# Mixture-of-experts blocks of a two-layer trunk on Trainium2: input rows loaded two blocks ahead and copied into place by GpSimd

## Chip, cores and metric

One Trainium2 chip, one core, float32 throughout. The metric is the time of the whole program on the device, in microseconds (us); less is better. The engines are named as the profile names them: PE (TensorE), DVE (VectorE), ACT (ScalarE), POOL (GpSimd) and SP (SyncE, which only issues DMAs here); a "q" behind a name is the engine's sequencer.

## The reference

Two layers of a diffusion backbone run over 128 context and 256 latent tokens of width 1024. Each layer is a mixer (attention in the first, long convolution in the second), a layer norm, a mixture of experts and a layer norm. What matters here is the mixture of experts, with 16 experts of inner width 512, two of which are chosen for each of the 384 tokens:

```
hg = t @ w_gate[e];  hu = t @ w_up[e]
act = silu(hg) * hu * comb[:, e]
y = sum_e act @ w_down[e]
```

An expert's three matrices are 2 MB each, so a layer reads 96 MB of them; the tokens are 1.5 MB.

## The kernel before

**Slots.** After the router, POOL scatters each token's row twice by indirect DMA (L469) into a DRAM tensor, slot_rows, at a place sorted by expert; each expert's rows are padded to blocks of BLK = 32. `table` holds where each expert's blocks begin, and its last entry is the number of blocks, which depends on the data. slot_rows was filled with zeros near the start of the program (L1217).

**The loop over blocks.** Each engine runs its own loop of that many trips, and they meet by semaphores alone.

- POOL (`pool_moe`) waits until PE has transposed the rows of a block (rowT_mm) and then loads the next block's 32 rows, as 64 half rows, from slot_rows into slot_in (L475). There is one such buffer.
- PE (`pe_moe`) waits for row_in and transposes slot_in into a PSUM bank (L733, in `rows_to_channels`); does the 64 gate and up matmuls of a block (L740); transposes the next block's rows while ACT and DVE make the activation; then does the 32 down matmuls (L747).
- ACT (`act_moe`) applies Silu (L1038, with a table load before it), and copies half of the result from PSUM into slot_out (L1041). Then it stores slot_out into slot_rows by two DMAs (L1045), over the rows that the block was read from.
- DVE (`dve_moe`) copies the transposed rows out of PSUM (L1114), multiplies and transposes the activation (L1119, L1121), and copies the other half of the result (L1135). L1041 and L1135 both wait for slot_stored: the store of the block before must have landed, since there is one slot_out.
- SP (`load_moe`) streams the weights through nine places of 2 MB, three experts deep (L416). A place is filled again when PE's last use of it is over. So an expert's loads are issued when the expert three before it is done.

**Around the loop.** In POOL's program, the wait for down_mm of the last expert but one and a small addition (L484) follow the loop, then `ln_rows` (four loads of 512 KB for the next layer norm, L440 to L442), waits for the last row load and the last store, an addition (L490), and six gathers of the result rows (L494). ACT's L953 and DVE's L982 to L988 work on what the gathers bring. POOL's L451 is a layer norm's addition.

Of the kernel before, what the change touches and what calls it, by code (L numbers as in the profile page):

```python
# [15 lines left out]
F32 = mybir.dt.float32  # L16
# [6 lines left out]
D = 1024  # L23
# [138 lines left out]
def trunk_program(nc, a, out):  # L162

    ctx = ExitStack()
    with ctx:
# [13 lines left out]
        idx = sb("idx", [P, 2 * NT], I32)  # L179
        table = sb("table", [1, NE + 1], I32)  # L180
        ada_bias = sb("ada_bias", [P, 512])
        bank = [ctx.enter_context(nc.psum_tensor(f"bank{i}", [P, 512], F32))[:, :] for i in range(8)]

        slots = nc.dram_tensor("slot_rows", [(MAX_BLOCKS + 2) * BLK, D], F32).ap()

# [80 lines left out]
        act_T = at(4096, FT, BLK)  # L266
        slot_out = at(4224, 512, rows=2 * BLK)
        SPARE = 7168
        picked = at(8192, NT, 2, D)
# [25 lines left out]
        def rt(k, *dims):  # L295
# [46 lines left out]
        rlog_mm, rscore, htok_mm, htok_act = [sem(n) for n in ("rlog_mm", "rscore", "htok_mm", "htok_act")]  # L342
        mask_rdy, pos_mm, table_rdy, idx_rdy, zero_rdy, zeroed, scattered, ln_first = [sem(n) for n in (
            "mask_ready", "pos_mm", "table_ready", "idx_ready", "zero_ready", "zeroed", "scattered", "rows_scaled")]
        MS = [{n: sem(f"{n}_{layer}") for n in (
            "row_in", "rowT_mm", "rowT", "gu_mm", "silu", "gated", "act", "down_mm", "evac_dve", "evac_act",
            "slot_stored")} for layer in range(2)]
# [113 lines left out]
        def pool_moe(pool, l):  # L461
            S = MS[l]
            pool.wait_ge(idx_rdy, 2 * (l + 1))
            pool.wait_ge(htok_act, 6 * (l + 1))
            if l == 0:
                pool.wait_ge(zeroed, 16 * ZERO_DMAS)
            for r in range(2):
                for t in range(NT):
                    pool.indirect_dma_start(slots[:, :], bass.IndirectOffsetOnAxis(ap=idx[:, r * NT + t:r * NT + t + 1], axis=0),  # L469
                                            h_tok[:, t, :], None).then_inc(scattered, 16)  # L470
            pool.wait_ge(table_rdy, l + 1)
            blocks = pool.value_load(table[0:1, NE:NE + 1], min_val=NE, max_val=MAX_BLOCKS)
            pool.wait_ge(scattered, 16 * 6 * (l + 1))
            def row_halves(block):
                pool.dma_start(slot_in, slots[bass.ds(block * BLK, BLK), :].rearrange("s (h c) -> (s h) c", h=2)).then_inc(S["row_in"], 16)  # L475

            row_halves(0)
            with pool.Fori(1, blocks + 1) as b:
                pool.wait_ge(S["rowT_mm"], b)
                row_halves(b)  # L480

            before_last = pool.value_load(table[0:1, NE - 1:NE], min_val=NE - 1, max_val=MAX_BLOCKS)
            pool.wait_ge(S["down_mm"], before_last)
            pool.tensor_tensor(idle, wsel[:, 0, 0:1], wsel[:, 0, 0:1], ALU.add).then_inc(idle_set, 1)  # L484
            pool.wait_ge(idle_set, 2 * l + 1)
            ln_rows(pool, 2 * l + 1)
            pool.wait_ge(S["row_in"], blocks * 16 + 16)
            pool.wait_ge(S["slot_stored"], blocks * 32 + 32)
            pool.wait_ge(S["rowT"], blocks + 1)
            pool.tensor_tensor(idle, wsel[:, 0, 0:1], wsel[:, 0, 0:1], ALU.add).then_inc(idle_set, 1)  # L490
            pool.wait_ge(idle_set, 2 * l + 2)
            for t in range(NT):
                for r in range(2):
                    pool.indirect_dma_start(picked[:, t, r, :], None, slots[:, :],  # L494
                                            bass.IndirectOffsetOnAxis(ap=idx[:, r * NT + t:r * NT + t + 1], axis=0)).then_inc(gathered[t], 16)
# [206 lines left out]
        def pe_moe(pe, l, first):  # L702
# [26 lines left out]
            def rows_to_channels():  # L729

                wait_counted(pe, S["row_in"], rows_due, 16)
                for j in range(4):
# [34 lines left out]

            rows_due = counter(pe, f"rows_due{l}", 16)
            rows_to_channels()
# [131 lines left out]
        MIX_DMAS = 3  # L901
        ZERO_STEP = 6
        ZERO_DMAS = (MAX_BLOCKS + 2) // ZERO_STEP
        CONST_ALL = 16 * 6
# [143 lines left out]
        def dve_moe(dve, link, l):  # L1048
# [58 lines left out]
            for r, oh in enumerate((oh0, oh1)):  # L1107
                link(dve.tensor_tensor(eq, oh, soff, ALU.mult))
                link(dve.tensor_reduce(slot_f[:, r, :], eq, AX, ALU.add))
                dve.tensor_copy(idx[:, r * NT:(r + 1) * NT], slot_f[:, r, :]).then_inc(idx_rdy, 1)  # L1110
            dve.wait_ge(table_rdy, l + 1)
            blocks = dve.value_load(table[0:1, NE:NE + 1], min_val=NE, max_val=MAX_BLOCKS)
# [11 lines left out]
            dve.sem_inc(S["evac_dve"], 1)  # L1124
            dve.wait_ge(S["rowT_mm"], 1)
            rows_in()
            with dve.Fori(0, blocks) as b:
                dve.wait_ge(S["silu"], b + 1)
                gated(b, 0)
                gated(b, 1)  # L1130
                dve.wait_ge(S["rowT_mm"], b + 2)
                rows_in()
# [71 lines left out]
        def gpsimd_program(pool):  # L1204
# [10 lines left out]
            rows = slots.rearrange("(b r) n -> r b n", r=BLK)  # L1215
            for b in range(0, MAX_BLOCKS + 2, ZERO_STEP):
                pool.dma_start(rows[:, b:b + ZERO_STEP, :],  # L1217
# [458 lines left out]
```

## Time and profile before

| what | value |
|---|---|
| device time, median of 3 runs | 1385.99 us (1384.95 to 1388.35) |
| device time of the profiled execution | 1387.69 us |
| its span, first to last instruction | 1386.0 us |
| granted clock of PE, mean | 0.884 |
| PE busy | 1025.2 us (74%) |
| DVE busy | 412.2 us (30%) |
| ACT busy | 262.3 us (19%) |
| POOL busy | 107.8 us (8%) |
| moved by DMA | 343.83 MB, 248 GB/s over the span |

A profile is one execution. Busy shares are means over stages with different limits; what a wait costs is read from the chain of work that ended last, which is followed back from the last instruction, at each step to what released it. A line such as `PE L733 MATMUL bank<-keep,arena` names engine, line, operation and the tensors written and read; slot_in, slot_out, slot_ahead and the other buffers of the loop all lie in `arena`. In a timeline, the brackets at a line's end hold how long the engine had been idle and what released it. Times are microseconds from the start of the span.

### The profile page before, as it was taken

The page shows a single profiled execution, that of the slowest core. Times are in us where ns is not written, and L with a number is a line of the kernel's source. Part 1 is how long each engine was busy: PE and PEld are TensorE (multiplying, and loading weights), DVE is VectorE, ACT ScalarE, POOL GpSimd, SP SyncE. Part 2 cuts the span into 40 slices and gives each one's busy share as a digit, 9 for nine tenths or more (in the row PEclk, how much of TensorE's full clock was granted, in tenths as well). Part 3 has the DMA queues.
Part 4 walks back from the last instruction along what each step waited for, and adds up shares of the span by engine and source line. Part 5 has one row for each costly group of instructions (what it writes and reads, how often), then busy time and mean ns, then how long its engine had stood idle before and what let it go on. Part 6 is the DMA issues. An engine that isn't in the chain of part 4 may idle for free.

```text
span 1386.0 us, 23542 instructions
## 1 busy us (share of the span) xinstructions
PE 1025.2 (74%) x9358; PEld 573.8 (41%) x9358; DVE 412.2 (30%) x1120; ACT 262.3 (19%) x456; POOL 107.8 (8%) x168
## 2 busy tenths in 40 slices
PE   1899996896368655778569999889748788876540
PEld 0444455645234323444235554435434444443220
DVE  0310128806211111112354234551631222111106
ACT  0401012502122211223122111110222222222111
POOL 1100001100200000000220000000010000000012
PEclk9999998996699878999879999999858999988785
DMA  9975334394396999993995104636421938799983
GB/s 322 372 255 182 129 117 150 120 426 167 121 386 231 390 411 404 401 349 128 348 377 217 61 16 139 240 122 262 163 93 36 369 129 328 275 396 404 411 338 136
DMA packets 78264, 343.83 MB, mean 248 GB/s; under 512 B 7783, under 2 KB 8362, under 8 KB 65917
## 3 DMA queue, kind: packets, MB, share of 16 engines
q1 hardware_dynamic: 57108, 289.16, 54.0%
q0 software_dynamic: 13152, 42.92, 9.0%
q10 hardware_dynamic: 7944, 10.88, 2.4%
q8 instruction: 47, 0.77, 0.2%
q14 instruction: 13, 0.10, 0.0%
HBM read 319.70 MB, written 23.23 MB: 247 GB/s over the span
## 4 chain that ended last, share of the span: by engine, by line
PE 43%; DMA 34%; DVE 11%; issue 6%; ACT 2%; SPq 2%; ACTq 1%; POOL 1%; POOLq 0%; DVEq 0%
DMA slot_rows<-arena 11%; PE bank L575 10%; PE bank L800 9%; PE bank L740 7%; DMA arena<-in_moe_w_up_dram 6%; DMA arena<-slot_rows 5%; DMA ring<-in_moe_w_up_dram 5%; DMA ring<-in_ada_w_dram 4%; PE bank L747 4%; PE bank L698 3%; DMA arena<-in_ln_b_dram 2%; PE bank L528 2%; SPq L1151 1%; PE bank L874 1%; PE bank L897 1%
## 5 line engine op out<-in xcount | busy, mean ns | idle before, releaser
L740 PE MATMUL bank<-ring,arena 128*32 128x256 f32 x3008 | 189.1, 408 | 35.0 <-DMA ring<-in_moe_w_up_dram 32.8
L740 PEld LDWEIGHTS bank<-ring,arena 128*32 128x32 f32 x3008 | 103.1, 119 | 116.8 <-issue 60.3
L575 PE MATMUL bank<-ring,hT 128*128 128x512 f32 x336 | 144.9, 593 | 1.0 <-ACT hT L933 1.0
L800 PE MATMUL bank<-hT,ring 128*128 128x384 f32 x384 | 124.6, 487 | 1.0 <-ACT hT L933 1.0
L747 PE MATMUL bank<-ring,arena 128*32 128x256 f32 x1504 | 105.7, 428 | 23.5 <-DVE arena L1121 23.5
L1119 DVE TENSOR_TENSOR arena<-arena,bank 128x64 f32<-128x64 f32 x134 | 27.0, 201 | 287.8 <-ACT arena L1038 287.8
L733 PE MATMUL bank<-keep,arena 64*128 64x64 f32 x276 | 31.9, 239 | 103.6 <-DMA arena<-slot_rows 103.6
L1038 ACT ACT_TABLE_LOAD x67 | 86.0, 1283 | 105.6 <-issue 97.5
L740 PE MATMUL bank<-arena 128*32 128x256 f32 x1280 | 82.7, 416 | 24.6 <-DMA arena<-in_moe_w_up_dram 24.6
L575 PEld LDWEIGHTS bank<-ring,hT 128*128 128x128 f32 x336 | 63.6, 190 | 80.5 <-issue 79.3
L800 PEld LDWEIGHTS bank<-hT,ring 128*128 128x128 f32 x384 | 72.7, 190 | 52.5 <-ACT hT L933 1.2
L528 PE MATMUL bank<-ring,small 128*32 128x256 f32 x768 | 52.7, 435 | 56.2 <-DMA ring<-in_ada_w_dram 54.9
L1135 DVE COPY arena<-bank 64x256 f32<-64x256 f32 x67 | 27.9, 416 | 177.2 <-DMA slot_rows<-arena 121.8
L1041 ACT ACTIVATE arena<-bank 64x256 f32<-64x256 f32 x67 | 25.5, 381 | 287.5 <-DMA slot_rows<-arena 181.8
L475 POOL DMA_DIRECT2D arena<-slot_rows x69 | 36.2, 525 | 552.7 <-PE bank L733 545.2
L733 PEld LDWEIGHTS bank<-keep,arena 64*128 64x128 f32 x276 | 23.2, 144 | 132.8 <-issue 132.8
L747 PEld LDWEIGHTS bank<-ring,arena 128*32 128x32 f32 x1504 | 48.6, 120 | 59.9 <-DVE arena L1121 27.6
L740 PEld LDWEIGHTS bank<-arena 128*32 128x32 f32 x1280 | 44.8, 121 | 60.7 <-issue 39.3
L528 PEld LDWEIGHTS bank<-ring,small 128*32 128x32 f32 x768 | 28.5, 125 | 78.9 <-issue 68.1
L747 PE MATMUL bank<-arena 128*32 128x256 f32 x640 | 48.6, 455 | 11.5 <-DVE arena L1121 11.5
L1114 DVE COPY arena<-bank 128x256 f32<-128x256 f32 x69 | 27.7, 401 | 55.8 <-PE bank L733 55.4
L698 PE MATMUL bank<-ring,arena 128*128 128x512 f32 x96 | 41.5, 593 | 1.3 <-DVE arena L1647 1.3
(285 smaller groups left out, 1014.1 us busy)
## 6 DMA issues: line engine op xcount, KB each, us to landing
ring<-in_ada_w_dram SPq DMA_DIRECT2D x24, 2048.0 KB, 15.2
ring<-in_moe_w_gate_dram SPq DMA_DIRECT2D x22, 2048.0 KB, 20.9
ring<-in_moe_w_up_dram SPq DMA_DIRECT2D x22, 2048.0 KB, 23.9
ring<-in_moe_w_down_dram SPq DMA_DIRECT2D x22, 2048.0 KB, 25.4
arena<-in_moe_w_gate_dram SPq DMA_DIRECT2D x10, 2048.0 KB, 24.0
arena<-in_moe_w_up_dram SPq DMA_DIRECT2D x10, 2048.0 KB, 29.3
arena<-in_moe_w_down_dram SPq DMA_DIRECT2D x10, 2048.0 KB, 29.6
ring<-in_ev_w_in_dram SPq DMA_DIRECT2D x7, 2048.0 KB, 15.7
```

Source lines behind the costliest of these rows:

```text
L475: pool.dma_start(slot_in, slots[bass.ds(block * BLK, BLK), :].rearrange("s (h c) -> (s h) c", h=2)).then_inc(S["row_in"], 16)
L528: pe.matmul(b[32 * j:32 * j + 32, 0:HALF], condT[:, 2 * k:2 * k + 32], slot8(chunks[j // 2])[:, k, j % 2 * HALF:j % 2 * HALF + HALF], star ...
L575: last = pe.matmul(bank[3 * (c % 2) + t], hT[:, k, t * P:(t + 1) * P], slot8(n)[:, k, :], start=k == 0, stop=k == KT - 1)
L698: last = pe.matmul(bank[2 * t + half], src[:, k, t * P:(t + 1) * P], slot8(n0 + half)[:, k, :], start=k == 0, stop=k == KT - 1)
L733: last = pe.transpose(bank[0][:, j * 2 * BLK:(j + 1) * 2 * BLK], slot_in[:, j * P:(j + 1) * P], ident[0:2 * BLK, 0:2 * BLK])
L740: last = pe.matmul(bank[1][q * BLK:(q + 1) * BLK, 0:HALF], slot_inT[:, k, :], both[:, :, k, q * P:(q + 1) * P], start=k == 0, stop=k == KT ...
L747: last = pe.matmul(bank[5][tile * BLK:(tile + 1) * BLK, 0:HALF], act_T[:, f, :], slot4(s + 2)[:, f, q * HALF:(q + 1) * HALF], start=f == 0 ...
L800: last = pe.matmul(bank[c % 3][:, 0:T], slot8(n)[:, k, (c % 4) * P:(c % 4 + 1) * P], hT[:, k, :], start=k == 0, stop=k == KT - 1)
L1038: act.activation(silu_g, bank[1][:, 0:P].rearrange("p (r f) -> p f r", f=FT), ACT.Silu).then_inc(S["silu"], 1)
L1114: return dve.tensor_copy(slot_inT.rearrange("p (h j) s -> p h j s", h=2), bank[0][:, 0:HALF].rearrange("p (j s h) -> p h j s", j=4, h=2)). ...
L1119: dve.tensor_tensor(act_rows[:, two, :], silu_g[:, two, :], up, ALU.mult).then_inc(S["gated"], 1)
L1135: dve.tensor_copy(slot_out[:, 0:HALF], bank[5][0:2 * BLK, 0:HALF]).then_inc(S["evac_dve"], 1)
```

## The change

Two buffers of 64x512, slot_ahead, take the row loads. The first two blocks are loaded before the loop. In each step POOL waits for the load of this block and for PE's transposes of the block before, does an addition on one column, copies the buffer into slot_in (row_rdy, which PE now waits for), waits for that copy, and issues the load of the block two further on into the same buffer. The loop is in pairs of blocks, so the number of trips is not the number of blocks: DVE works out blocks / 2 rounded down, plus 1, after the table, into `trips`. rowT_mm starts from 1, so DVE's waits on it are one higher. slot_rows is two blocks longer, and the zero fill goes in eleven steps of four blocks instead of seven of six.

```diff
@@ -178,10 +178,11 @@
...
         table = sb("table", [1, NE + 1], I32)
+        trips = sb("trips", [1, 1], I32)
         ada_bias = sb("ada_bias", [P, 512])
...
-        slots = nc.dram_tensor("slot_rows", [(MAX_BLOCKS + 2) * BLK, D], F32).ap()
+        slots = nc.dram_tensor("slot_rows", [(MAX_BLOCKS + 4) * BLK, D], F32).ap()
@@ -265,6 +266,7 @@
...
         slot_out = at(4224, 512, rows=2 * BLK)
+        slot_ahead = [at(5376, 512, rows=2 * BLK), at(5888, 512, rows=2 * BLK)]
         SPARE = 7168
@@ -340,10 +342,10 @@
...
         rlog_mm, rscore, htok_mm, htok_act = [sem(n) for n in ("rlog_mm", "rscore", "htok_mm", "htok_act")]
-        mask_rdy, pos_mm, table_rdy, idx_rdy, zero_rdy, zeroed, scattered, ln_first = [sem(n) for n in (
-            "mask_ready", "pos_mm", "table_ready", "idx_ready", "zero_ready", "zeroed", "scattered", "rows_scaled")]
+        mask_rdy, pos_mm, table_rdy, idx_rdy, zero_rdy, trips_rdy, zeroed, scattered, ln_first = [sem(n) for n in (
+            "mask_ready", "pos_mm", "table_ready", "idx_ready", "zero_ready", "trips_ready", "zeroed", "scattered", "rows_scaled")]
         MS = [{n: sem(f"{n}_{layer}") for n in (
-            "row_in", "rowT_mm", "rowT", "gu_mm", "silu", "gated", "act", "down_mm", "evac_dve", "evac_act",
+            "row_in0", "row_in1", "row_rdy", "rowT_mm", "rowT", "gu_mm", "silu", "gated", "act", "down_mm", "evac_dve", "evac_act",
             "slot_stored")} for layer in range(2)]
@@ -470,21 +472,31 @@
...
             blocks = pool.value_load(table[0:1, NE:NE + 1], min_val=NE, max_val=MAX_BLOCKS)
+            pool.wait_ge(trips_rdy, l + 1)
+            pairs = pool.value_load(trips[0:1, 0:1], min_val=NE // 2 + 1, max_val=MAX_BLOCKS // 2 + 1)
             pool.wait_ge(scattered, 16 * 6 * (l + 1))
-            def row_halves(block):
-                pool.dma_start(slot_in, slots[bass.ds(block * BLK, BLK), :].rearrange("s (h c) -> (s h) c", h=2)).then_inc(S["row_in"], 16)
-
-            row_halves(0)
-            with pool.Fori(1, blocks + 1) as b:
-                pool.wait_ge(S["rowT_mm"], b)
-                row_halves(b)
+
+            def rows_ahead(block, odd):
+                pool.dma_start(slot_ahead[odd], slots[bass.ds(block * BLK, BLK), :].rearrange("s (h c) -> (s h) c", h=2)).then_inc(S[f"row_in{odd}"], 16)
+
+            rows_ahead(0, 0)
+            rows_ahead(1, 1)
+            with pool.Fori(0, pairs) as pair:
+                for odd in range(2):
+                    pool.wait_ge(S[f"row_in{odd}"], pair * 16 + 16)
+                    pool.wait_ge(S["rowT_mm"], pair * 2 + (odd + 1))
+                    pool.tensor_tensor(idle, wsel[:, 0, 0:1], wsel[:, 0, 0:1], ALU.add)
+                    pool.tensor_copy(slot_in, slot_ahead[odd]).then_inc(S["row_rdy"], 1)
+                    pool.wait_ge(S["row_rdy"], pair * 2 + (odd + 1))
+                    rows_ahead(pair * 2 + (odd + 2), odd)
...
             ln_rows(pool, 2 * l + 1)
-            pool.wait_ge(S["row_in"], blocks * 16 + 16)
+            for odd in range(2):
+                pool.wait_ge(S[f"row_in{odd}"], pairs * 16 + 16)
             pool.wait_ge(S["slot_stored"], blocks * 32 + 32)
@@ -728,7 +740,7 @@
...
-                wait_counted(pe, S["row_in"], rows_due, 16)
+                wait_counted(pe, S["row_rdy"], rows_due, 1)
                 for j in range(4):
@@ -765,7 +777,8 @@
...
-            rows_due = counter(pe, f"rows_due{l}", 16)
+            rows_due = counter(pe, f"rows_due{l}", 1)
+            pe.sem_inc(S["rowT_mm"], 1)
             rows_to_channels()
@@ -899,8 +912,8 @@
...
         MIX_DMAS = 3
-        ZERO_STEP = 6
-        ZERO_DMAS = (MAX_BLOCKS + 2) // ZERO_STEP
+        ZERO_STEP = 4
+        ZERO_DMAS = (MAX_BLOCKS + 4) // ZERO_STEP
         CONST_ALL = 16 * 6
@@ -1108,6 +1121,11 @@
...
                 dve.tensor_copy(idx[:, r * NT:(r + 1) * NT], slot_f[:, r, :]).then_inc(idx_rdy, 1)
+            pairs_f = rt(12, 1)
+            link(dve.tensor_scalar(pairs_f, base[:, NE:NE + 1], 0.5, 0.75, ALU.mult, ALU.add))
+            link(dve.tensor_scalar(pairs_f, pairs_f, ROUND, None, ALU.add))
+            link(dve.tensor_scalar(pairs_f, pairs_f, ROUND, None, ALU.subtract))
+            dve.tensor_copy(trips[0:1, :], pairs_f[0:1, :]).then_inc(trips_rdy, 1)
             dve.wait_ge(table_rdy, l + 1)
@@ -1122,13 +1140,13 @@
...
             dve.sem_inc(S["evac_dve"], 1)
-            dve.wait_ge(S["rowT_mm"], 1)
+            dve.wait_ge(S["rowT_mm"], 2)
             rows_in()
...
                 gated(b, 1)
-                dve.wait_ge(S["rowT_mm"], b + 2)
+                dve.wait_ge(S["rowT_mm"], b + 3)
                 rows_in()
@@ -1213,7 +1231,7 @@
...
             rows = slots.rearrange("(b r) n -> r b n", r=BLK)
-            for b in range(0, MAX_BLOCKS + 2, ZERO_STEP):
+            for b in range(0, MAX_BLOCKS + 4, ZERO_STEP):
                 pool.dma_start(rows[:, b:b + ZERO_STEP, :],
...
```

## Rows read from the trace of the kernel before

**Rows 1.** The page's part 4, the chain that ended last, shares of the span by line.

```profile
DMA slot_rows<-arena 11%; PE bank L575 10%; PE bank L800 9%; PE bank L740 7%; DMA arena<-in_moe_w_up_dram 6%; DMA arena<-slot_rows 5%; DMA ring<-in_moe_w_up_dram 5%; DMA ring<-in_ada_w_dram 4%; PE bank L747 4%; PE bank L698 3%; DMA arena<-in_ln_b_dram 2%; PE bank L528 2%; SPq L1151 1%; PE bank L874 1%; PE bank L897 1%
```

**Rows 2.** Who waited for whom: us in total, times, longest.

```profile
DVE arena L1135 <- DMA slot_rows<-arena: 121.8, 33, 5.6
...
PE bank L733 <- DMA arena<-slot_rows: 103.6, 36, 19.8
```

**Rows 3.** DMA issues: times, KB each, median us from issue to landing.

```profile
slot_rows<-arena ACTq DMA_DIRECT2D x134, 64.0 KB, 6.4
```

**Rows 4.** Timeline, 645 to 653, no weights in flight: start us, us, instruction.

```profile
645.10 0.46 PE L733 MATMUL bank<-keep,arena 64*128 64x64 f32 x4
...
645.80 0.24 DVE L1121 STREAM_TRANSPOSE arena<-arena 128x64 f32<-128x64 f32 x1
...
646.11 1.93 PE L747 MATMUL bank<-ring,arena 128*32 128x256 f32 x32 [0.54 <-DVE arena L1121]
...
646.36 0.39 DVE L1114 COPY arena<-bank 128x256 f32<-128x256 f32 x1
647.86 3.64 PE L740 MATMUL bank<-ring,arena 128*32 128x256 f32 x64
...
651.42 0.46 PE L733 MATMUL bank<-keep,arena 64*128 64x64 f32 x4
```

**Rows 5.** The chain in order of time, 376 to 430: start us, us, what.

```profile
388.43 8.54 DMA arena<-slot_rows
...
401.48 0.43 DVE arena L1135
...
428.67 0.43 DVE arena L1135
```

**Rows 6.** Timeline, 376 to 403, VectorE's L1135.

```profile
380.69 0.42 DVE L1135 COPY arena<-bank 64x256 f32<-64x256 f32 x1 [1.46 <-PE bank L747]
...
390.01 0.42 DVE L1135 COPY arena<-bank 64x256 f32<-64x256 f32 x1 [1.78 <-DMA slot_rows<-arena]
```

**Rows 7.** Windows: us, busy of PE, PEld, DVE, ACT, POOL, PEclk, DMA share, GB/s.

```profile
1190.00:1330.00 140.00, 94.57 (x1324) 49.45 (x1316) 20.69 (x79) 25.61 (x40) 7.06 (x15) 0.83 1.00 402
```

**Rows 8.** POOL's groups: busy us, mean ns, idle before.

```profile
L451 POOL TENSOR_TENSOR x<-arena 128x1024 f32<-128x1024 f32 x3 | 9.0, 2991 | 73.7 <-DVE arena L1018 73.7
...
L1213 POOL MEMSET arena<- 32x1024 f32 x1 | 0.9, 943 | 42.5 <-PE bank L1268 42.5
```

**Rows 9.** The chain in order of time, 340 to 700.

```profile
364.33 3.69 issue
...
552.35 7.80 DMA arena<-slot_rows
...
564.14 0.43 DVE arena L1135
...
601.83 8.77 DMA arena<-slot_rows
```

**Rows 10.** The row loads of layer 1, by their line, 1000 to 1386.

```profile
L475 POOL DMA_DIRECT2D arena<-slot_rows x35: 522/522/580, 1038.0 to 1327.6; - x35
```

**Rows 11.** Timeline of PE, 1285 to 1348.

```profile
1321.37 5.16 PE L740 MATMUL bank<-arena 128*32 128x256 f32 x64 [6.92 <-DMA arena<-in_moe_w_up_dram]
...
1338.28 5.24 PE L740 MATMUL bank<-ring,arena 128*32 128x256 f32 x64 [8.87 <-DMA ring<-in_moe_w_up_dram]
```

**Rows 12.** Timeline, 1324 to 1386, POOL, ScalarE and VectorE.

```profile
1330.01 1.20 POOL L440 DMA_DIRECT2D arena<-gate_rows  x2 [0.30 <-POOL small L484]
...
1356.82 1.15 ACT L953 ACTIVATE arena<-arena,small 128x1024 f32<-128x1024 f32 x1 [9.90 <-DMA arena<-slot_rows,idx]
...
1359.43 1.22 DVE L983 TENSOR_TENSOR arena<-arena 128x1024 f32<-128x1024 f32 x1
...
1371.68 3.31 POOL L451 TENSOR_TENSOR x<-arena 128x1024 f32<-128x1024 f32 x1 [14.26 <-DVE arena L1018]
1372.83 3.25 DVE L983 TENSOR_TENSOR arena<-arena 128x1024 f32<-128x1024 f32 x1
```

## The prediction

> **What bounds the kernel now.** I read the chain of work that ended last first, because busy shares say nothing about a wait. The experts' loop puts three things on it [rows 1]: the weight DMAs, the DMA that stores a block's output rows (slot_rows<-arena, 11% of the span) and, with 5%, the DMA that loads a block's input rows (arena<-slot_rows), which is what the change attacks. The waits give the same contest from the engines' side [rows 2]: TensorE stood idle 103.6 us before the transposes of L733 for that load, but VectorE's L1135, the copy of the result into slot_out, stood 121.8 us for the store before it. Both are round trips of one buffer through one DMA; a store lands 6.4 us after its issue in the median [rows 3].
>
> Next the timeline of a block while no weights are in flight [rows 4]. The 64 gate and up matmuls take 3.64 us, the transposes of the next rows 0.46, the activation ends in L1121, the down matmuls take 1.93, and from L733 of one block to that of the next (645.10, 651.42) it is 6.3 us. PE waits for no rows there, and nothing can be won.
>
> While weights are in flight the row load takes 8.5 us [rows 5] and the store as long: L1135 runs at 380.69 and 390.01 [rows 6], 9.3 us apart, and from 401.48 to 428.67 the chain makes three rounds of store and L1135 in 27.2 us, 9.06 each [rows 5]. A round of rows (0.45 of transposes, 0.55 of issue, 7 to 8.5 of DMA) is 8.0 to 9.5 us. So **two loops of nearly equal length run side by side**, and the change opens only the one that is mostly hidden by the other.
>
> Last the windows [rows 7]: from 1190 to 1330 the DMA share is 1.01 at 402 GB/s. There the weights' own bytes set the pace, and a faster block merely waits longer.
>
> **Part by part.** The base is the profiled execution, 1387.69 us for a span of 1386.0; the median of the runs shown is 1385.99, so 1.7 lower, and I count changes against either.
>
> 1. *Start of each layer's loop.* Rows of block 0 used to land where PE takes them. Now POOL waits, does a one-column addition (0.2), a gap and the 64x512 copy before PE may start. The copy is not in the trace. Lower end: half of the 1024-column memset of L1213, 0.47 us. Upper end: half of L451's addition of 1024 columns, 2.99 in the mean, so 1.5 [rows 8]. A copy reads one operand where the addition reads two, so I take the middle, 1.0. With 0.2 and some 0.3 of gaps: **+1.5 us a layer, +3.0 together** (2.0 to 4.0). The Trainium skill (GPSIMD Engine Reference, on its per-element model) has 769 ns for a tight loop over 512 elements; by that the two starts would cost 2.5 instead of 3.0.
>
> 2. *First contended blocks, layer 0.* Row load 388.43 + 8.54 holds PE until L1135 can only run at 401.48 [rows 5]. With rows ready the store loop ends the wait: 390.01 plus a round of 9.3 [rows 6] is 399.3. **-2.2.** From 401.48 on the chain is stores alone; nothing more comes there.
>
> 3. *Around 552.* The load 552.35 + 7.80 delays L1135 to 564.14 [rows 9]. The transposes before that load began 1.05 before 552.35, so by the block of [rows 4] (L733, 1.0 later L747, its 1.93 and 0.1) L1135 ran at 554.3; a store round of 9.06 on is 563.4, and with rows at hand nothing else is late. **-0.8.** Again stores follow.
>
> 4. *From 601.83 on*, four row loads in a row are on the chain, 8.77 us the first [rows 9]. But in that stretch the results wait for stores too, and the block period ahead is bounded by the store round; I follow the blocks one by one with the store landings held fixed and get half a microsecond at the end of it. **-0.5** (0 to -2).
>
> 5. *Layer 1.* One row load is on the chain, near 1190, just when the DMA share reaches 1.01 and stays there for 140 us [rows 7]: **0**. The later start counts in full, as it delays the release of the first ring buffers.
>
> 6. *POOL's tail, layer 1.* This is the step that is moved. Layer 1 had 35 row loads [rows 10], so 34 blocks; an even number makes one trip more than PE uses, and its copy waits for the last transposes (end of the L740 of 1338.28, 1343.5 and 0.45 [rows 11]). All that POOL has behind it waits as well: the wait for down_mm, L484, and the four 512 KB loads of ln_rows, which were issued from 1330.01 [rows 12]. They move to 1343.9 + 1.5 + 0.6 for the last row load + 1.1 for the table value and L484, so 1347.1. Two effects. They leave the way of the last weights: the last L740 began 16.9 us after the one before it [rows 11], where 6.55 MB for an expert and its rows at 402 GB/s [rows 7] is 16.3: **-0.6**. And 2.1 MB stand in POOL's queue ahead of the gathers: at 402 GB/s 5.2 us, from about 1348.5 to 1353.7; two gathers of 512 KB and a landing of 2 us later it is 1358.3, where ScalarE's first L953 began at 1356.82 [rows 12]: **+2.0** after allowing for the pace of the later gathers (0, if they hide, to +5.2, if all of it stands ahead).
>
> 7. *The rest.* Eleven zero fills of 512 KB replace seven of 768 KB: 0.26 MB more, 0.65 us at 402 GB/s in a stretch with weights, of which I take **+0.3**. VectorE has four more small operations and POOL one more table value before the loop; they lie beside POOL's wait of 3.69 us for the scatters [rows 9], and cost about 0.5 us if that cover went. In the steady loop POOL does copy, wait and issue in some 2.3 us of the 6.3 of a block, and PE needs the copy only at the end of the next block: nothing. A load is issued one transposition plus 1.6 us later and is wanted two blocks on, over 12 us, against 8.8 for the longest load: PE's wait for rows should go almost whole. Layer 0 has 33 blocks, so no extra trip.
>
> Sum: +3.0 -2.2 -0.8 -0.5 -0.6 +2.0 +0.3 = **+1.2**, so 1388.9 for a profiled execution and 1387 for a median. What is late in place of the rows is the store before.
>
> **Rivals.** *Faster, because stores get quicker.* Row loads would be issued about 2 us earlier in a block than now, and if a store thereby took 0.8 us less, some 18 of the 33 waits of L1135 [rows 2] would shrink, if those in saturated stretches like that of [rows 7] are left out: -14, 1373. For it: both use the same DMA engines and overlap. Against: one row load per store still overlaps it. 0.17.
>
> *Faster, PE's wait is the price.* If the 103.6 us that L733 stood idle [rows 2] were on the path, the kernel would come to 1283. Against: the chain has 5% for that DMA, and each of its pieces ends beside a store. 0.03.
>
> *Slower, the copy holds up VectorE.* L983 took 3.25 us beside POOL's L451 of 3.31, and 1.22 without it [rows 12]. If POOL's copy, which comes as L1121 and L1114 run [rows 4], blocked them for its full 1.0 us, the second L1121 would end 0.35 us after the down matmuls want it; over some 17 blocks at the 6.3 us pace that is +6, 1393. It decides from a delay of about 0.65 us on. 0.10. The Trainium skill (SBUF — State Buffer, "Who interferes with whom") says that a VectorE instruction contends with a GpSimd one that reads SBUF if it has two SBUF inputs or runs in a 2-port mode; L983 has two, in agreement with its 3.25, and the loop's operations have one, so by that rule this rival gives 0 in place of +6.
>
> *Slower, the moved ln_rows.* If the gathers wait for the whole 5.2 us in POOL's queue and the copy is at its upper end (+1.0), it is 1387 + 3.2 + 1.0 = 1391.2. It decides when the gathers come over 5 us late. 0.13.
>
> **Chances.** A measurement of this kernel tells about 0.3%, 4.2 us, from no change. The forecast, 1382 to 1391, has 0.57; faster 0.17 + 0.03 = 0.20; slower 0.10 + 0.13 = 0.23. The range leaves out the far end of both sides: 1374 to 1395.
>
> **What the profile would show.** Right: L733's wait for rows near zero, now for a POOL copy of about 1 us; L1135's wait for stores grown, above 140 us; slot_rows<-arena with more of the chain, arena<-slot_rows gone; the first L740 of each layer 1.5 us later; ln_rows issued near 1347. Wrong: a store median well under 6.4 us, a block without weights in flight at other than 6.3 us, or L1135 waiting no longer than before while the layers end many microseconds sooner.

## The result, and the profile after

The changed kernel takes 1399.96 us (median of 4 runs, 1396.3 to 1401.74) where the kernel before, run beside it, took 1387.17 (1384.95 to 1390.42): a ratio of 1.0087, with an interval of 1.0057 to 1.0117. Two more sets gave 1.0037 and 1.0067 (below). It is slower, by 5 to 13 us, and the forecast of no change is wrong. The profiled run took 1396.3 us for a span of 1394.6, 8.6 us above the one before.

The page's part 4, the chain that ended last, by line:

```profile
DMA slot_rows<-arena 15%; PE bank L587 10%; PE bank L813 9%; PE bank L752 8%; DMA arena<-in_moe_w_up_dram 6%; DMA ring<-in_moe_w_up_dram 5%; DMA ring<-in_ada_w_dram 5%; PE bank L759 4%; PE bank L710 3%; DMA arena<-in_ln_b_dram 2%; PE bank L540 2%; ACTq L1058 1%; SPq L1169 1%; PE bank L887 1%; PE bank L910 1%
```

The row load arena<-slot_rows, 5% in [rows 1], is gone from it. The store slot_rows<-arena had 11% and has 15%. The two together were 16% and are 15%: the chain has changed its route, and the two DMAs have kept their share of it.

The waits of the changed kernel (us in total, times, longest). L745 is the transposes' line (before L733), L752 gate and up, L759 the down matmuls, L1139 the transposed activation, L1153 and L1054 the two copies of the result into slot_out, L489 POOL's new copy:

```profile
POOL small L488 <- PE bank L745: 463.7, 66, 17.2
...
ACT arena L1054 <- DMA slot_rows<-arena: 198.6, 35, 7.2
DVE arena L1153 <- DMA slot_rows<-arena: 155.6, 35, 6.0
...
PE bank L759 <- DVE arena L1139: 98.1, 67, 4.7
...
PE bank L745 <- POOL arena L489: 41.1, 2, 20.7
```

TensorE no longer waits for rows inside the loop: the 41.1 us before its transposes are the two starts of the layers, which lie in the 103.6 us of [rows 2] too. The idle time has gone one step down the block. In the kernel before this line was

```profile
PE bank L747 <- DVE arena L1121: 35.0, 40, 2.9
```

so before the down matmuls it was 35.0 us in 40 times and is 98.1 in 67; before transposes and down matmuls together it was 103.6 + 35.0 = 138.6 and is 41.1 + 98.1 = **139.2 us**. The copy of the result waits 155.6 us for the store before it, where [rows 2] have 121.8: an earlier result reaches a slot_out that is no earlier free.

Why a late store holds TensorE at the down matmuls shows in ScalarE's order of work. From the timeline at 624 (L1054 is its copy of the result, L1051 the Silu of the next block):

```profile
624.05 0.38 ACT L1054 ACTIVATE arena<-bank 64x256 f32<-64x256 f32 x1 [5.93 <-DMA slot_rows<-arena]
...
626.06 1.28 ACT L1051 ACT_TABLE_LOAD   x1 [1.62 <-issue]
627.35 0.28 ACT L1051 ACTIVATE arena<-bank 128x128 f32<-128x128 f32 x1
```

ScalarE stands in its copy until the store has landed, then issues the next store, loads its table and only then applies Silu. The next block's gate/up was done at 624.1, its down matmuls begin at 628.22. So the store's wait reaches TensorE through ScalarE, whether or not the rows are there. (Silu before the copy was not tried.)

The chain in order of time from 376 to 430 (start us, us, what), the stretch of [rows 5, 6]:

```profile
383.15 8.54 DMA slot_rows<-arena
391.71 0.43 DVE arena L1153
...
392.83 8.33 DMA slot_rows<-arena
401.18 0.43 DVE arena L1153
...
402.29 7.37 DMA slot_rows<-arena
...
410.79 7.70 DMA slot_rows<-arena
...
419.62 9.11 DMA slot_rows<-arena
428.76 0.43 DVE arena L1153
```

Each store is followed by the next result's copy, and that by the next store; gate/up, transposes and down matmuls hide behind them. The last copy in it starts at 428.76; before it was at 428.67.

POOL's new instructions, by line (busy us, mean ns | idle before), and the store in the list of DMA issues, where [rows 3] have 6.4 us:

```profile
L489 POOL COPY arena<-arena 64x512 f32<-64x512 f32 x70 | 42.0, 601 | 0.0
...
L488 POOL TENSOR_TENSOR small<-small 128x1 f32<-128x1 f32 x70 | 13.2, 188 | 466.9 <-PE bank L745 463.7 <-DMA arena<-slot_rows 3.3
```

```profile
slot_rows<-arena ACTq DMA_DIRECT2D x134, 64.0 KB, 6.1
```

And a block without weights in flight, from the timeline of 640 to 656, to stand beside [rows 4]:

```profile
643.45 0.60 POOL L489 COPY arena<-arena 64x512 f32<-64x512 f32 x1
643.47 0.24 DVE L1139 STREAM_TRANSPOSE arena<-arena 128x64 f32<-128x64 f32 x1
...
643.77 1.93 PE L759 MATMUL bank<-ring,arena 128*32 128x256 f32 x32 [0.54 <-DVE arena L1139]
...
649.09 0.46 PE L745 MATMUL bank<-keep,arena 64*128 64x64 f32 x4
...
655.41 0.46 PE L745 MATMUL bank<-keep,arena 64*128 64x64 f32 x4
```

The period is 6.32 us as before. L489 runs in the same 0.6 us as L1139, and L1139 still takes 0.24 with the down matmuls 0.54 behind it: with no weights in flight the copy costs nothing.

**Stages.** The first and last instructions of the stages, read from the timelines of several profiles, give this table (us; the mean where there are several profiles, with their ends):

```
                               before, 2 profiles     after, 3 profiles
scatters -> transposes, L0     13.7                   14.9
loop of layer 0 (33 blocks)    294.3 (293.3, 295.2)   297.6 (295.7 to 298.6)
untouched stretch up to L1     352.1 (352.0, 352.2)   354.8 (353.8 to 356.5)
scatters -> transposes, L1     13.8                   14.7
loop of layer 1 (34 blocks)    305.9 (304.4, 307.3)   305.7 (302.9 to 307.4)
last result copy -> gathers    3.6                    6.8
span                           1387.0                 1397.5
```

A loop is counted from the first gate/up matmul to the start of the last result copy. Three things are plain: the layers start 1.2 and 0.9 us later, the gathers of layer 1 come 3.2 us later behind the last result, and the loops between won nothing. That is 5.3 us of the 10.5. The rest is in layer 0's loop and in a stretch whose instructions the change doesn't touch. These two rows are the loosest of the table: the run before_late_lnrows below, which is the kernel before up to the end of layer 1, has 293.7 us for that loop and 354.1 for that stretch, and exact_trips, which is the changed kernel up to there, 295.6 and 353.8.

Part of the difference has a place. From the first gather of layer 0 to TensorE's second group of matmuls on in_ada_w, the weights that are loaded behind the experts', it is 36.3, 36.4 and 37.1 us in the three profiles with the old loop and 38.8, 38.9 and 39.0 in the three of the changed kernel. The chain waits there for the first of these weights: 18.0 us before, 22.1 after.

```profile
665.16 17.95 DMA ring<-in_ada_w_dram
```

```profile
669.16 22.14 DMA ring<-in_ada_w_dram
```

Why that load lands later, no run shows.

### The profile page after: what moved, and what is told of

It reads as the page before. It is cut to its first block, busy times and chain, and to the rows that moved or that the text cites. A ratio compares the mean times of both kernels' runs of the same rounds, so it can differ in the third digit from the quotient of the medians.

```text
span 1394.6 us, 23687 instructions
## 1 busy us (share of the span) xinstructions
PE 1027.1 (74%) x9358; PEld 573.2 (41%) x9358; DVE 410.6 (29%) x1128; ACT 262.6 (19%) x456; POOL 163.5 (12%) x317
## 4 chain that ended last, share of the span: by engine, by line
PE 43%; DMA 34%; DVE 11%; issue 5%; ACT 3%; ACTq 1%; SPq 1%; POOL 1%; POOLq 0%; DVEq 0%
DMA slot_rows<-arena 15%; PE bank L587 10%; PE bank L813 9%; PE bank L752 8%; DMA arena<-in_moe_w_up_dram 6%; DMA ring<-in_moe_w_up_dram 5%; DMA ring<-in_ada_w_dram 5%; PE bank L759 4%; PE bank L710 3%; DMA arena<-in_ln_b_dram 2%; PE bank L540 2%; ACTq L1058 1%; SPq L1169 1%; PE bank L887 1%; PE bank L910 1%
## 5 line engine op out<-in xcount | busy, mean ns | idle before, releaser
L752 PE MATMUL bank<-ring,arena 128*32 128x256 f32 x3008 | 192.1, 413 | 37.8 <-DMA ring<-in_moe_w_up_dram 35.6
L752 PEld LDWEIGHTS bank<-ring,arena 128*32 128x32 f32 x3008 | 104.2, 120 | 122.1 <-issue 67.3
L759 PE MATMUL bank<-ring,arena 128*32 128x256 f32 x1504 | 104.1, 423 | 61.4 <-DVE arena L1139 61.4
L752 PE MATMUL bank<-arena 128*32 128x256 f32 x1280 | 83.8, 420 | 24.2 <-DMA arena<-in_moe_w_up_dram 24.2
L1153 DVE COPY arena<-bank 64x256 f32<-64x256 f32 x67 | 27.9, 417 | 205.6 <-DMA slot_rows<-arena 155.6
L759 PEld LDWEIGHTS bank<-ring,arena 128*32 128x32 f32 x1504 | 47.9, 118 | 98.0 <-DVE arena L1139 67.8
L1054 ACT ACTIVATE arena<-bank 64x256 f32<-64x256 f32 x67 | 25.6, 382 | 287.5 <-DMA slot_rows<-arena 198.6
L759 PE MATMUL bank<-arena 128*32 128x256 f32 x640 | 48.0, 451 | 36.7 <-DVE arena L1139 36.7
L752 PEld LDWEIGHTS bank<-arena 128*32 128x32 f32 x1280 | 45.0, 122 | 61.3 <-issue 40.2
L488 POOL TENSOR_TENSOR small<-small 128x1 f32<-128x1 f32 x70 | 13.2, 188 | 466.9 <-PE bank L745 463.7
L745 PE MATMUL bank<-keep,arena 64*128 64x64 f32 x276 | 32.1, 237 | 41.1 <-POOL arena L489 41.1
L745 PEld LDWEIGHTS bank<-keep,arena 64*128 64x128 f32 x276 | 22.6, 140 | 68.8 <-issue 68.8
L480 POOL DMA_DIRECT2D arena<-slot_rows x74 | 39.0, 528 | 55.3 <-POOL arena L489 46.8
L759 PEld LDWEIGHTS bank<-arena 128*32 128x32 f32 x640 | 21.2, 124 | 54.0 <-DVE arena L1139 39.5
```

The source lines that it names most:

```text
L480: pool.dma_start(slot_ahead[odd], slots[bass.ds(block * BLK, BLK), :].rearrange("s (h c) -> (s h) c", h=2)).then_inc(S[f"row_in{odd}"], 16)
L745: last = pe.transpose(bank[0][:, j * 2 * BLK:(j + 1) * 2 * BLK], slot_in[:, j * P:(j + 1) * P], ident[0:2 * BLK, 0:2 * BLK])
L752: last = pe.matmul(bank[1][q * BLK:(q + 1) * BLK, 0:HALF], slot_inT[:, k, :], both[:, :, k, q * P:(q + 1) * P], start=k == 0, stop=k == KT ...
L759: last = pe.matmul(bank[5][tile * BLK:(tile + 1) * BLK, 0:HALF], act_T[:, f, :], slot4(s + 2)[:, f, q * HALF:(q + 1) * HALF], start=f == 0 ...
L1054: act.activation(slot_out[:, HALF:2 * HALF], bank[5][2 * BLK:4 * BLK, 0:HALF], ACT.Copy).then_inc(S["evac_act"], 1)
L1153: dve.tensor_copy(slot_out[:, 0:HALF], bank[5][0:2 * BLK, 0:HALF]).then_inc(S["evac_dve"], 1)
```

## Experiments

**The changed kernel again**, twice (no edit).

> The changed kernel once more, as the yardstick for the others. Every theory: between 1396 and 1402 us, 9 to 15 us above the kernel before; its profile shows again first scatter to first transposes some 1.0 to 1.2 us longer a layer, and the last copy of the result to the first gather 6.8 us instead of 3.6 in layer 1.

Measured: 1397.22 us (12 runs) against 1390.34 (35 runs), ratio 1.0037 (1.0015 to 1.0060). The time is in the range; 7 us above the kernel before is less than the 9 to 15 expected. The two stages came again as expected (14.9 and 14.8 us at the starts, 6.7 at the end).

> The changed kernel again, on another set of runs. Theory A (two first copies of 1.1 us and the moved ln_rows with 3.2 us, no gain in the loops): 4 to 8 us above the kernel before. Rival B (a cost of 10 us or more, of which half is in the loops): 10 us or more above it.

Measured: 1398.25 us (7 runs) against 1388.66 (24 runs), ratio 1.0067 (1.0044 to 1.0090). With 9.6 us it lies between the two theories (4 to 8, and 10 or more) and decides for neither. The slowdown is real in all three sets; its size moves between 5 and 13 us.

**The kernel before again**, as a measure of what such a comparison tells.

> The kernel before, run as if it were an experiment: it shows what a difference of nothing looks like in twelve runs. Every theory: a ratio within 0.3% of 1. Its profile is a second sample of each stage: stages in which nothing is changed should differ from the first profile's by no more than some 2 us.

Measured: 1389.17 us (12 runs), 1.0007 (0.9984 to 1.0029), so an interval of 0.2% on either side. Its layer 1 loop took 307.3 us where the first profile has 304.4: a single profile says nothing about 3 us in a loop.

**No extra trip in layer 1.** POOL makes 17 pairs for 33 blocks, as the changed kernel does, and 17 instead of 18 for 34. PE's last transposes, whose result nothing uses, are let through by one more raise of row_rdy behind POOL's loop.

```diff
+            pool.sem_inc(S["row_rdy"], 1)
...
-            link(dve.tensor_scalar(pairs_f, base[:, NE:NE + 1], 0.5, 0.75, ALU.mult, ALU.add))
+            link(dve.tensor_scalar(pairs_f, base[:, NE:NE + 1], 0.5, 0.25, ALU.mult, ALU.add))
```

> POOL's loop makes no trip more than there are rows to copy (17 pairs in both layers), so ln_rows of layer 1 is issued under the last expert again. Theory A (the moved ln_rows stands before the last block's store and the gathers): 3 us less than the changed kernel, last copy of the result to first gather back at 3.6 us, 1393 to 1398. Rival B (the cost lies in the loop, in POOL's copy beside VectorE or in later row loads): no change beyond 1 us. Rival C (ln_rows merely takes time from the last weights instead): the layer's last weights land 1 us later and at most 2 us are won.

Measured: 1393.25 us (12 runs), 1.0026 (0.9997 to 1.0055), 4.0 less than the changed kernel run beside it; 3 were expected. The end of layer 1 is where the profiles differ. First the kernel before, 1346 to 1351:

```profile
1346.56 0.42 DVE L1135 COPY arena<-bank 64x256 f32<-64x256 f32 x1 [1.46 <-PE bank L747]
1347.18 0.80 ACTq L1045 DMA_DIRECT2D slot_rows<-arena  x2
1349.44 0.19 POOL L490 TENSOR_TENSOR small<-small 128x1 f32<-128x1 f32 x1 [17.19 <-DMA slot_rows<-arena]
1350.15 1.01 POOL L494 DMA_INDIRECT arena<-slot_rows,idx  x1 [0.53 <-POOL small L490]
```

Then the changed kernel's timeline, 1349 to 1359:

```profile
1349.34 0.60 POOL L489 COPY arena<-arena 64x512 f32<-64x512 f32 x1
...
1352.00 1.12 POOL L442 DMA_DIRECT2D arena<-gate_rows  x2 [0.47 <-POOL small L495]
1352.33 0.80 ACTq L1058 DMA_DIRECT2D slot_rows<-arena  x2
...
1353.63 0.53 POOL L444 DMA_DIRECT2D arena<-in_ln_b_dram  x1
1357.82 0.19 POOL L502 TENSOR_TENSOR small<-small 128x1 f32<-128x1 f32 x1 [3.66 <-DMA slot_rows<-arena]
1358.53 1.03 POOL L506 DMA_INDIRECT arena<-slot_rows,idx  x1 [0.52 <-POOL small L502]
```

And the same place without the extra trip:

```profile
1339.14 1.12 POOL L442 DMA_DIRECT2D arena<-gate_rows  x2 [0.30 <-POOL small L496]
...
1355.17 0.80 ACTq L1059 DMA_DIRECT2D slot_rows<-arena  x2
...
1357.41 0.19 POOL L503 TENSOR_TENSOR small<-small 128x1 f32<-128x1 f32 x1 [16.11 <-DMA slot_rows<-arena]
1358.32 1.03 POOL L507 DMA_INDIRECT arena<-slot_rows,idx  x1 [0.72 <-POOL small L503]
```

With the extra trip the 2 MB of ln_rows are issued in the same microsecond as the last store (1352.00 and 1352.33), and 5.5 us pass from that store's issue to L502, which waits for it (1352.33 to 1357.82); without it 2.2 (1355.17 to 1357.41). From the last result copy to the first gather it is 6.8 us against 3.8. The gathers are not held by ln_rows in POOL's queue: from the first of them to ScalarE's first use of what they bring (L953, L966 here) it is 6.8 us (1358.53 to 1365.37), and 6.7 in the kernel before (1350.15 to 1356.82).

**The kernel before with ln_rows late**: that step alone.

```diff
             pool.wait_ge(S["down_mm"], before_last)
+            if l == 1:
+                pool.wait_ge(S["rowT_mm"], blocks + 1)
```

> The kernel before with that one step of the change alone: in layer 1 POOL waits for the last transposes before ln_rows. Theory A: 3 us slower than before, 1389 to 1392, with last copy of the result to first gather 6.5 to 7 us. Rivals B and C: within 1 us of the kernel before.

Its timeline at the same place:

```profile
1347.83 0.53 POOL L442 DMA_DIRECT2D arena<-in_ln_b_dram  x1
...
1348.82 0.86 ACTq L1047 DMA_DIRECT2D slot_rows<-arena  x2
1354.49 0.19 POOL L492 TENSOR_TENSOR small<-small 128x1 f32<-128x1 f32 x1 [6.14 <-DMA slot_rows<-arena]
```

The store again takes 5.7 us to L492, and the stage is 6.8 us: the +3.2 is reproduced without any other part of the change. The total doesn't show it, 1391.08 us (12 runs), 1.0002 (0.9976 to 1.0028): 3.2 us is 0.23%, inside that interval. So the mechanism is shown in the trace, and its price in the total isn't resolved: 1391.08 suits the 3 us expected as well as the rivals' nothing.

**Rows of block 0 straight into slot_in.** The first block keeps its old path; the buffers ahead begin with blocks 1 and 2. This takes away the first copy and, as the count of pairs falls to 16 and 17, one pair in each layer.

```diff
-            rows_ahead(0, 0)
-            rows_ahead(1, 1)
+            pool.dma_start(slot_in, slots[0:BLK, :].rearrange("s (h c) -> (s h) c", h=2)).then_inc(S["row_first"], 16)
+            rows_ahead(1, 0)
+            rows_ahead(2, 1)
...
-                    rows_ahead(pair * 2 + (odd + 2), odd)
+                    rows_ahead(pair * 2 + (odd + 3), odd)
...
-            link(dve.tensor_scalar(pairs_f, base[:, NE:NE + 1], 0.5, 0.75, ALU.mult, ALU.add))
+            link(dve.tensor_scalar(pairs_f, base[:, NE:NE + 1], 0.5, -0.25, ALU.mult, ALU.add))
```

> The rows of the first block go straight to slot_in and are not copied; trips are exact as well. Theory A, with 1.2 us a layer for the first copy: 2 to 2.5 us under exact_trips, 1391 to 1396; what then stays above the kernel before, 4 to 8 us, is from neither the start nor the tail. Rival B: the same as exact_trips within 1 us, still 9 us or more above the kernel before.

> Rows ahead with neither of the two costs (the first block's rows go straight to slot_in, exact trips), again. Theory A: within 3 us of the kernel before, since the store paces the loops. If it is 4 us or more under it, the loops have a gain of their own from rows ahead.

Measured: 1386.47 (12 runs), 0.9981 (0.9959 to 1.0004), and 1387.43 (12 runs), 0.9989 (0.9970 to 1.0008). Scatters to transposes is 13.6 us in both layers, last copy to gathers 3.8. With the start and the tail mended, the rows loaded two blocks ahead are worth nothing that a measurement tells from no change. Against the changed kernel it gains 10.8 us both times, twice what its two stages account for (2 x 1.2 and 3.0), and it is 6.8 us under exact_trips where 2 to 2.5 were expected.

The traces show a third effect of the edit. With 16 pairs in place of 17, POOL is done earlier in layer 0 too, and ln_rows of that layer (2 MB) is issued at 654.13, 10 us before the load of in_ada_w starts and not 4 as in the changed kernel (664.99 and 669.16). Those weights then land after 12.7 us (13.2 in the second profile) where the changed kernel has 22.1:

```profile
664.58 12.74 DMA ring<-in_ada_w_dram
```

The stretch from layer 0's gathers to layer 1's scatters is 350.5 and 348.9 us for 354.8. That is some 5 us, the size of what is missing. No run moves ln_rows of layer 0 alone, so this part is read from the traces and not tested by itself, and in these two profiles layer 0's loop is shorter as well (below).

**Open the other loop, or both.** First by removal: the store of the blocks' results is left out (the same semaphore is raised at once), so the experts' part is missing from what these two kernels compute.

```diff
-                for h in range(2):
-                    act.dma_start(slots[bass.ds(b * BLK, BLK), h * 512:(h + 1) * 512], slot_out[h * BLK:(h + 1) * BLK, :]).then_inc(S["slot_stored"], 16)
+                act.sem_inc(S["slot_stored"], 32)
```

> The kernel before without the stores of the blocks' results (the output then lacks the experts' part): what the row loads alone cost. Theory D (two loops of nearly equal length): taking only the store away wins little, since the row load still paces the contended blocks: 5 to 15 us under the kernel before. Rival E (the store alone paces the loop, the row load is slack): 25 us or more.

> The changed kernel with exact trips, again without the stores. Theory D: with both loops open a contended block takes 6.3 us, so this is at least 5 us under before_no_store, and 20 us or more under the kernel before, until the weights bound it. Rival E: equal to before_no_store. Rival F (rows ahead do not help even where nothing else waits, because weights bound the layers): both equal, and each within 10 us of the kernel before.

Measured: on the kernel before 1370.17 us (4 runs), 0.9833 (0.9797 to 0.9869); on the changed one with exact trips 1328.82 (4 runs), 0.9551 (0.9513 to 0.9588). Without stores, rows ahead are worth 41 us; with them, nothing. The first came 22 us under the kernel before, where 5 to 15 were expected, but that comparison isn't clean. The layers end sooner because no last store is waited for (last copy to gathers 1.4 and 1.3 us for 7.1 and 3.6), and layer 1, whose input is another one, has 33 blocks in place of 34. In layer 0, with its 33 blocks, the loop takes 290.0 us for 294.3: opening the store's loop alone is worth 4 us there. With both open it takes 262.7.

Then with all the work in place, by a second result buffer: slot_out alternates between two places, each with its own semaphore, and ACT and VectorE go in pairs (with one empty step where the count of blocks is odd).

```diff
-        slot_out = at(4224, 512, rows=2 * BLK)
+        slot_outs = [at(4224, 512, rows=2 * BLK), at(6400, 512, rows=2 * BLK)]
...
-                act.wait_ge(S["slot_stored"], b * 32 + 32)
+                act.wait_ge(S[f"slot_stored{odd}"], two * 32 + 32)
```

> The kernel before with two slot_out buffers, so that a result waits for the store two blocks back; one row buffer as before; an odd count of blocks costs one empty step in layer 0 (about 4 us). Theory D: the row load still paces, 0 to 8 us under the kernel before. Rival E: 20 us or more under it.

Measured: 1390.28 us (10 runs), 0.9986 (0.9956 to 1.0016), 2 us under the kernel before, as expected of two equal loops. The second buffer does its work, since no copy of the result waits for a store any more, and the time stays. Its waits of TensorE (L738 is the transposes' line, L752 the down matmuls) and its chain by line:

```profile
PE bank L738 <- DMA arena<-slot_rows: 117.1, 40, 19.7
...
PE bank L752 <- DVE arena L1146: 15.5, 29, 0.6
```

```profile
DMA arena<-slot_rows 17%; PE bank L580 10%; PE bank L813 9%; PE bank L745 8%; DMA arena<-in_moe_w_up_dram 5%; DMA ring<-in_ada_w_dram 4%; PE bank L752 4%; DMA ring<-in_moe_w_down_dram 3%; PE bank L703 3%; DMA arena<-in_ln_b_dram 2%; DMA ring<-in_moe_w_up_dram 2%; PE bank L533 2%; PE bank L738 1%; SPq L1178 1%; PE bank L887 1%
```

This is the mirror of the change: here the store is off the chain and the row load has 17%; there the row load is off it and the store has 15%.

> Rows two blocks ahead, exact trips and two slot_out buffers. Theory D: both loops are opened, so it is the first version under the kernel before, 1370 to 1382, and at least 5 us under before_two_outs. Rival F: 1387 or more.

> All that was found put together: rows two blocks ahead, the first block's rows not copied, exact trips, and two slot_out buffers. Theory D: 0 to 3 us under exact_two_outs, 1343 to 1347, some 45 us under the kernel before. If the first copy counts for nothing once the weights pace the layers: the same as exact_two_outs, 1346.6.

Measured: 1346.64 us (4 runs), 0.9671 (0.9639 to 0.9703), far below the 1370 to 1382 expected, so the theory had the direction right and the size at less than half; and with the first rows loaded straight, **1343.81 us (6 runs, 1342.64 to 1349.02), 0.9687 (0.9660 to 0.9714)**. The last computes all that the reference does and beats both kernels. Its waits of TensorE (L756 transposes, L763 gate/up, L770 down matmuls) and its chain by line:

```profile
PE bank L763 <- DMA ring<-in_moe_w_up_dram: 56.1, 11, 8.7
...
PE bank L756 <- DMA arena<-slot_rows: 38.8, 2, 19.7
PE bank L770 <- DVE arena L1174: 34.3, 63, 0.6
```

```profile
DMA ring<-in_moe_w_up_dram 14%; PE bank L763 13%; PE bank L594 11%; PE bank L836 9%; PE bank L770 6%; DMA ring<-in_moe_w_down_dram 5%; DMA ring<-in_ada_w_dram 4%; PE bank L717 3%; DMA arena<-in_ln_b_dram 2%; PE bank L547 2%; PE bank L729 1%; SPq L1206 1%; PE bank L910 1%; PE bank L933 1%; ACT arena L1079 1%
```

Neither the row load nor the store has 1% of it any more. The wait before the down matmuls is 34.3 us in 63 times, 0.54 each, the activation's own length; what PE waits for inside the experts is the weights. From the first gate/up to the first gather, layer 0 takes 278.4 us instead of 302.3 and layer 1 289.9 instead of 308.0, 42 together.

The four cases side by side:

```
                     one slot_out     two
rows one block at    1                0.9986 (0.9956 to 1.0016)
a time
rows two ahead       0.9981, 0.9989   0.9687 (0.9660 to 0.9714)
(first_direct)
```

## Why the prediction was wrong

**The diagnosis held.** "Two loops of nearly equal length run side by side", and "what is late in place of the rows is the store before": the table above is that sentence measured. The announced signs came: L733's wait for rows left the loop, L1135's wait for stores is 155.6 us (above 140), slot_rows<-arena has more of the chain, arena<-slot_rows none, a block without weights in flight stays at 6.32 us. What failed are the terms, nearly all in one direction. The step that failed first is the following of the blocks in steps 2 to 4, with the landings of the stores and TensorE's own times held fixed. It gave -3.5 us for layer 0's loop, and that loop came out 3.3 us longer (297.6 for 294.3). The second is in step 6, what the moved ln_rows slows. And 2.7 us lie in the stretch between the layers, for which the sum has no term.

*Step 1, start of each layer's loop.* Forecast +1.5 a layer, measured +1.2 and +0.9. The mechanism is right. The term mis-sized is the copy: 0.60 us, not 1.0, near the lower bound (the memset's 0.47) and far from the addition's. The 769 ns that the Trainium skill (GPSIMD Engine Reference, on its per-element model) gives for a tight loop over 512 elements were nearer than my middle, and still above what the trace has.

*Step 2, first contended blocks, -2.2.* It came at its place, at about half its size. From the first result copy to the third it was 401.48 - 380.69 = 20.8 us and is 401.18 - 381.97 = 19.2; from the first to the sixth 428.67 - 380.69 = 48.0 and 428.76 - 381.97 = 46.8. In the means of two and three profiles it is -1.3 at the third and -1.2 at the sixth. That the sixth copies stand at the same time (428.67, 428.76) is because the first comes 1.3 us later in this profile: its first gate/up group took 6.41 us for 5.13 (4.93 and 6.16 in the other two).

*Step 3, around 552, -0.8.* From 554.34 to 564.14 it was 9.8 us and is now (553.20 to 562.75) 9.55: -0.25, which is nothing beside the other profiles (8.8 before, 10.2 and 9.9 after). In that stretch the gate/up matmuls of one block start 3.5 us earlier than before (560.34 for 563.79), its down matmuls 2.2 (566.76 for 568.97), and its result is copied only 1.0 earlier (571.62 for 572.66): half of the lead is spent in front of the down matmuls, half in front of slot_out, which waits for the store.

*Step 4, from 601.83 on, -0.5.* Here the sign was wrong. The changed kernel goes from 0.3 us ahead to 4.0 behind between 615 and 640. One piece of it, PE's timeline:

```profile
624.03 0.46 PE L745 MATMUL bank<-keep,arena 64*128 64x64 f32 x4
628.22 3.64 PE L759 MATMUL bank<-arena 128*32 128x256 f32 x32 [3.73 <-DVE arena L1139]
631.63 4.88 PE L752 MATMUL bank<-ring,arena 128*32 128x256 f32 x64
```

and the same stretch in windows (columns as in [rows 7]):

```profile
622.00:624.40 2.40, 2.40 (x44) 1.33 (x36) 0.35 (x1) 0.35 (x1) 0.00 (x0) 1.00 1.06 364
...
628.20:631.80 3.60, 3.58 (x36) 1.75 (x40) 0.62 (x3) 0.00 (x0) 0.00 (x0) 0.50 1.05 368
...
637.40:639.40 2.00, 1.95 (x36) 1.21 (x40) 0.66 (x3) 0.00 (x0) 0.91 (x2) 1.00 0.00 0
```

A block's idle time used to be split before the transposes and before the down matmuls and now stands in one piece of 3.73 us; behind it the down matmuls take 3.64 us instead of the 1.93 of [rows 4], at a granted clock of 0.50 (1.2 GHz) where the block before had 1.00 (2.4 GHz), and gate/up 4.88 instead of 3.64. I held PE's times fixed when I followed the blocks, and they are not fixed. But the clock is not shown to be the cause. All down matmuls together take 154.3 and 154.2 us in the two profiles before and 152.1, 153.4 and 156.7 after, and the kernel before has a group of 3.60 us in the same stretch. What the trace does show is that the three rounds before 637.45 take 9.0, 9.5 and 9.2 us (down matmuls at 609.71, 618.71, 628.22, 637.45), each with the store's landing and ScalarE's sequence in it, where those of the kernel before, paced by row loads that got shorter (8.77, 6.96, 6.37, 5.44 us on its chain), take 8.2, 7.6 and 6.7. And first_direct, with the same loop, took 293.6 and 290.4 us for layer 0. **Why layer 0's loop is some 3 us longer in the changed kernel, and why in_ada_w behind it lands later, stays open.** It is half of the slowdown.

*Step 5, layer 1's loop, 0.* Right: 305.7 against 305.9.

*Step 6, POOL's tail.* The step is right: the copy of the extra trip waits for the last transposes, and ln_rows is issued 3.4 us behind them (3.6 forecast), at 1352.0 and not at 1347.1, because the transposes came later. The -0.6 for the last weights didn't come: the last two gate/up groups are 16.9 us apart in both kernels (1325.68 and 1342.58 in the changed one). The +2.0 was +3.2, and the failed step is its reason, "2.1 MB stand in POOL's queue ahead of the gathers". What the 2 MB slow is the last store, and that holds L502 and with it every gather. The step "who else has a transfer in flight at that time" was missing: I moved a 2 MB issue and looked only behind it in its own queue.

*Step 7, the rest, +0.3.* The scatters begin at 355.6 to 357.6 us against 357.0: the smaller zero fills cost nothing that can be seen.

*The rivals.* "Stores get quicker" is refuted as a gain: the median landing went from 6.4 to 6.1 us, but the stores on the chain that took over 5 us, those with weights in flight, took 7.9 in the mean (19) and take 8.1 (26). "PE's wait is the price" is refuted; and yet opening that loop together with the other gave 42 us, so the wait was the price of two loops, not of one. "The copy holds up VectorE" is refuted by L1139 and by 6.32; by the rule of the Trainium skill (SBUF — State Buffer, "Who interferes with whom") it gave 0, and the trace agrees. "The moved ln_rows" had its price of 3.2 right by luck: it has the gathers wait in POOL's queue, and they wait for the store. It ended on the right side at 1391.2, with half of the slowdown missing.

*The numbers.* Of the sum, +3.0 was +2.1, the four gains of -4.1 did not come, and +2.0 was +3.2: 5.3 us where I wrote +1.2, before the 3.3 of the loop and the 2.7 of the stretch. The 5.3 alone would have been 1391, inside the range. The range closed at 1395 because it let the three loop terms fail only to zero: no bound was put on a loop that comes out longer. (The DMA share of [rows 7] is 1.00, not 1.01; nothing hangs on it.) By ratio on the base of 1385.99 the three sets give 1391, 1395 and 1398.

## What to carry to other kernels

Where a loop has two round trips of one buffer each through the same DMAs, and their rounds are nearly equal, a second buffer for one of them is worth nothing and for both it is worth the whole: here 0%, 0% and 3.1%. An engine that works in order, as ScalarE here between its copy and its Silu, can carry such a wait to another engine. Ask of every such edit what the freed engine waits for next, and open that too, or don't start. And an issue that moves in time is to be priced by every transfer in flight at its new place, above all by a small store that a whole stage waits for.

## What the runs showed of the hardware that was not expected

A 64x512 fp32 copy on GpSimd took 0.60 us (599 to 625 ns in 70 of them), 1.2 ns a column, where its 128x1024 addition has 2.9 [rows 8]. A last store of 128 KB, 2.2 us from its issue to the instruction that waits for it, took 5.5 when 2 MB of loads were issued on another queue in the same microsecond, and 5.7 when they had been issued just ahead of it. And the granted clock can fall behind a gap: after 3.73 us of idleness in one piece, 32 down matmuls ran at 0.50 and took 3.64 us; a block earlier, after 3.22 us of it, they took 1.93.
